# Even mixing part of a two-layer recurrent decoder: where the state sums over values and the pair sums stand in TensorE's order

## The chip, the cores and the metric

The kernel runs on one core of a Trainium2 chip. The metric is the device time of one execution in microseconds (us), less is better. Engines are named as the profile names them: PE is TensorE (PEld its weight loads), DVE is VectorE, ACT is ScalarE, POOL is GpSimd, SP the engine that issues most transfers.

## What is computed

A prompt of 2048 positions and a sample group of 8 x 8 positions go through two layers that share all weights. The even layer runs retention heads and RWKV-7 heads side by side from one input projection; both feed one output projection. Only the RWKV part touches the change:

```python
def rwkv7_recurrence(r, log_decay, k, v, kk, a, S0):
    def step(S, inp):
        r_t, lw_t, k_t, v_t, kk_t, a_t = inp
        s_kk = jnp.einsum('bhvk,bhk->bhv', S, kk_t)
        S = (S * jnp.exp(lw_t)[:, :, None, :] - s_kk[..., None] * (kk_t * a_t)[:, :, None, :]
             + v_t[..., None] * k_t[:, :, None, :])
        return S, jnp.einsum('bhvk,bhk->bhv', S, r_t)
...
    kk = l2norm(hd(kr * k_k))
...
    y = y + jnp.sum(r * kr * r_k, -1, keepdims=True) * vr
```

The squared lengths for `l2norm` and the sums over r * kr * r_k are sums over the 64 channels of a head: the kernel calls them pair sums, since two heads share the 128 partitions of a channel block.

## The kernel before

Four phases run one after the other: `project_phase` for the even layer, `mix_even_phase`, `project_phase` for the odd layer, `mix_odd_phase`. The change is in `mix_even_phase`.

There the sequence is cut into 17 tiles of 128 positions (PT = 16 is the index of the last, the sample tile). The recurrence inside a tile is written as a triangular system. Its inverse is built by doubling, in levels of 2, 4, 8, 16, 32 and 64; at each level PE makes X (`level_X`), DVE masks or copies it, PE makes T (`level_T`), ACT copies it out. The work is a software pipeline written out by hand: each engine walks through the same `STEPS`, a tuple (p, t, n, m, q) of tiles one apart. In one step tile p is projected out (`project`, eight pieces of six matmuls of 512 columns), tile t = p + 1 is solved and updates the state, the inverse of tile n = t + 1 is built, tile m = n + 1 gets its factors, sums and keys, and tile q = m + 1 its low-rank input. Tiles outside 0 to 16 are None, so the first steps have no p; in those, `keep_clock(count)` issues dummy matmuls on the identity where the pieces of `project` would be.

Every engine executes its list in order. Engines wait for one another by semaphores (`await_(engine, name, tile)`). PSUM is eight banks with the names A_, B_, C_, D_, BX, BY and BC (two banks); several functions take turns on each.

What the change touches in PE's list of a step, in the order of the kernel before:

- `level_T(n, 2)`, `solve(t)` (inverse times right side, into B_), `state_of_values(t)` (keys times values, the first half of the state update, into D_, four column blocks for each half of the partitions), `level_X(n, 4)`, `project(p, 0)`, `outputs_of_solved(t)` (waits for `wv_ready`, DVE's scaled copy of what `solve` made), `state_of_solved(t)` (the second half of the state update, accumulated on the first in D_), `level_T(n, 4)`.
- `project(p, 5)`, `turn_factors(m)` (twelve transposes into A_, B_, D_), `level_T(n, 32)`, `project(p, 6)`, `sums(m)` (pair sums into D_), `project(p, 7)`, `turn_sums(m)` (turns the copied sums, into D_), then `ret_scores`, `level_X(n, 64)`, `key_scores(m)` (into C_ and D_), `level_T(n, 64)`, `ret_out`, `low_rank`, `ret_delta`, `turn_mix(t)`, and the next step begins with `right_side`, `level_X(n, 2)`, `outputs_of_values`, `level_T(n, 2)`.

On ACT, `token_major(m)` copies the three turned banks to SBUF (tokB, tokK, tokV, the last from D_; event `tok_written`), then comes `level(n, 32)`, then `copy_sums(m)` (event `sums_copied`). On DVE `lengths(m)` takes what `turn_sums` made (event `lengths_ready`).

Of the kernel before, what the change touches and what calls it, by code (L numbers as in the profile page):

```python
# [8 lines left out]
ACT = mybir.ActivationFunctionType  # L9
# [3 lines left out]
P = 128  # L13
# [4 lines left out]
PT = SEQ // P  # L18
# [664 lines left out]
Q = 32  # L683
# [47 lines left out]
def mix_even_phase(nc, t_in, out):  # L731
# [6 lines left out]
    with ctx:  # L738
        def sb(n, shape):
            return ctx.enter_context(nc.sbuf_tensor(f"me_{n}", shape, F32))  # L740
# [20 lines left out]
        pair = sb("pair", [P, Q])  # L761
# [66 lines left out]
        head_sums = z[:, 0:2, :]  # L828
# [14 lines left out]
        A_, B_, C_, D_, BX, BY, BC = bk[3], bk[4], bk[2], bk[6], bk[7], bk[1], (bk[0], bk[5])  # L843
# [68 lines left out]
        def await_(eng, name, n):  # L912


            if n >= 0:
                eng.wait_ge(E[name], n + 1)
# [278 lines left out]
        def _(act):  # L1195
            def A(o, i, f, **kw):
                return nc.scalar.activation(o, i, f, **kw)
# [87 lines left out]

            def copy_sums(m):
                await_(act, "pair_sums_ready", m)
                A(head_sums, D_[:, 0:2 * P].rearrange("p (k c) -> p k c", k=2), ACT.Copy).then_inc(E["sums_copied"], 1)

            def level(n, b):  # L1290
                if level_count(n, b) is None:
# [423 lines left out]
        def _(pe):  # L1715
            def mm(o, l, r, start=True, stop=True):
                return nc.tensor.matmul(o, l, r, start=start, stop=stop)  # L1717

            def turn(o, i):
                return nc.tensor.transpose(o, i, ident)  # L1720

            def keep_clock(count):

                for _ in range(count):
                    mm(BC[0][:, 0:P], ident, ident)
# [51 lines left out]
            def state_of_values(t):  # L1779
                await_(pe, "mixT_written1", t - 1)  # L1780
                for b in range(4):
                    for half in range(2):
                        p0 = 64 * half
                        o = D_[p0:p0 + 64, b * WN:(b + 1) * WN]
                        mm(o, tokK[t % 2][:, b, p0:p0 + 64], tokV[t % 2][:, 2 * b + half, :], start=b == 0, stop=False)
# [8 lines left out]
            def state_of_solved(t):  # L1794
                for b in range(4):
                    for half in range(2):
                        p0 = 64 * half
                        last_op = mm(D_[p0:p0 + 64, b * WN:(b + 1) * WN], tokB[t % 2][:, b, p0:p0 + 64], wv[:, 2 * b + half, :], start=False, stop=b == 3)
                        if b == 3:
                            last_op.then_inc(E[f"delta{half}_ready"], 1)  # L1800
# [78 lines left out]
            def receptance_scores(n):  # L1879
                await_(pe, "mga_read", n)  # L1880
                low_side(n, 1, (A_, B_), "g2")
# [34 lines left out]
            def sums(m):  # L1916
                await_(pe, "squares_ready", m)
                await_(pe, "bonus_in", m)
                await_(pe, "tok_written", m)
                for k, src in enumerate((sq, z)):  # L1920
                    for b in range(4):
                        last_op = mm(D_[b * Q:(b + 1) * Q, k * P:(k + 1) * P], pair[:], src[:, b, :])
                last_op.then_inc(E["pair_sums_ready"], 1)

            def turn_sums(m):
                await_(pe, "sums_copied", m)
                for k in range(2):
                    last_op = turn(D_[:, k * P:(k + 1) * P], head_sums[:, k, :])
                last_op.then_inc(E["sums_ready"], 1)
# [114 lines left out]
            for p, t, n, m, q in STEPS:  # L2044
                if m == 0:
                    pe.wait_ge(s_c[1], 16 * N_C[1])
                last_step = p == PT
                if t is not None:
                    right_side(t)
                if n == 0:  # L2050
                    keep_clock(8)
                if n is not None:
                    level_X(n, 2)
                if t is not None:
                    outputs_of_values(t)
                if n == 0:
                    keep_clock(12)
                if n is not None:
                    level_T(n, 2)
                if t is not None:  # L2060
                    solve(t)
                    if t < PT:
                        state_of_values(t)
                if n is not None:
                    level_X(n, 4)
                if p is not None and not last_step:
                    project(p, 0)
                elif p is None and n is not None:
                    keep_clock(4)
                if t is not None:  # L2070
                    outputs_of_solved(t)
                    if t < PT:
                        state_of_solved(t)
                if n == 0:
                    keep_clock(8)
                if n is not None:
                    level_T(n, 4)
                if p is not None and not last_step:
                    project(p, 1)
                elif p is None and n is not None:  # L2080
                    keep_clock(4)
                if n is not None:
                    key_side(n, "a")
                    level_X(n, 8)
                if p is not None and not last_step:
                    project(p, 2)
                elif p is None and n is not None:
                    keep_clock(6)
                if n is not None:
                    key_side(n, "b")  # L2090
                    level_T(n, 8)
                if p is not None and not last_step:
                    project(p, 3)
                elif p is None and n is not None:
                    keep_clock(4)
                if t == PT:
                    for r in range(2):
                        sample_ret_state(1, r)
                if n is not None:
                    level_X(n, 16)  # L2100
                    receptance_scores(n)
                    turn_q_k(n)
                    if n == 0:
                        keep_clock(8)
                    level_T(n, 16)
                if p is not None and not last_step:
                    project(p, 4)
                elif p is None and n is not None:
                    keep_clock(4)
                if t == PT:  # L2110
                    sample_wk_state(0)
                if n is not None:
                    level_X(n, 32)
                if p is not None and not last_step:
                    project(p, 5)
                elif p is None and n is not None:
                    keep_clock(4)
                if m == 0:
                    keep_clock(24)
                if m is not None:  # L2120
                    turn_factors(m)
                if n is not None:
                    level_T(n, 32)
                if p is not None and not last_step:
                    project(p, 6)
                elif p is None and n is not None:
                    keep_clock(4)
                if t == PT:
                    sample_wk_state(1)
                if m == 0:  # L2130
                    keep_clock(5)
                if m is not None:
                    sums(m)
                if p is not None and not last_step:
                    project(p, 7)
                elif p is None and n is not None:
                    keep_clock(4)
                if t == PT:
                    sample_wk_state(2)
                if m is not None:  # L2140
                    turn_sums(m)
                if n is not None:
                    ret_scores(n)
                    level_X(n, 64)
                if m is not None:
                    key_scores(m)
                if n is not None:
                    level_T(n, 64)
                    ret_out(n)
                if q is not None:  # L2150
                    low_rank(q)
                if n is not None and n < PT:
                    ret_delta(n)
                if t is not None:
                    turn_mix(t)
                if t == PT:
                    sample_wk_state(3)
                if last_step:
                    for part in range(KD):
                        project(p, part)  # L2160
# [1238 lines left out]
```

## Time and profile before

| what | value |
|---|---|
| time, median of 3 runs | 3091.2 us (3082.86 to 3097.23) |
| profiled execution, its own time | 3089.68 us |
| its span | 3087.9 us, 85694 instructions |
| PE busy over the span | 2990.2 us (97%) |
| DVE / ACT / POOL busy | 1917.3 / 994.2 / 486.3 us |
| mean granted clock of TensorE | 0.982 |

The span is what the trace covers; the execution's own time is 1.8 us more. The even mixing phase lies between about 706 and 1546 us of the span. A busy PE in these rows means that a matmul was in flight; since matmuls overlap, the distance from one start to the next says more than the duration.

### The profile page before, as it was taken

What the parts mean: (1) busy time and instruction counts of PE and PEld (TensorE: products, weight loads), DVE (VectorE), ACT (ScalarE), POOL (GpSimd) and SP (SyncE); (2) the same over time, 40 slices, a digit from 0 to 9 for tenths busy, and PEclk for the clock granted to TensorE, in tenths of its full rate; (3) what the DMA queues carried; (4) which work ended last, traced back from release to release, by engine and by line L of the source; (5) the groups of instructions that cost most, each with busy time, mean ns of one, the idle gap of its engine ahead of it and who ended that gap; (6) DMA issues with size and microseconds to landing.
All of it is one profiled execution on the core that took longest, in us unless ns stands there. A gap on an engine that the chain in (4) does not pass through costs nothing. (4 is left out here: it accounts for less than half of the span.)

```text
span 3087.9 us, 85694 instructions
## 1 busy us (share of the span) xinstructions
PE 2990.2 (97%) x37108; PEld 2713.4 (88%) x37108; DVE 1917.3 (62%) x3976; ACT 994.2 (32%) x2170; POOL 486.3 (16%) x503
## 2 busy tenths in 40 slices
PE   9999999997999999999989999999996999999998
PEld 9999999996888888888789999999995788788886
DVE  4322244445777777777444266776765788788886
ACT  4221100003344344333166122222223344444441
POOL 0000000002343343333300000000001111111112
PEclk9999999998999999999899999999998999999999
DMA  6431122215233343333342222122114223333333
GB/s 217 142 91 69 60 91 69 69 57 182 76 121 103 114 121 113 117 121 124 104 171 90 82 73 77 61 77 77 61 64 154 84 84 98 93 97 97 98 105 130
DMA packets 216617, 311.45 MB, mean 101 GB/s; under 512 B 33449, under 2 KB 156081, under 8 KB 216113
## 3 DMA queue, kind: packets, MB, share of 16 engines
q1 hardware_dynamic: 203904, 260.76, 26.3%
q0 software_dynamic: 7872, 28.95, 3.1%
q10 hardware_dynamic: 4464, 16.25, 1.9%
q8 instruction: 294, 4.82, 0.7%
q14 instruction: 83, 0.67, 0.1%
HBM read 210.18 MB, written 95.72 MB: 99 GB/s over the span
## 5 line engine op out<-in xcount | busy, mean ns | idle before, releaser
L619 PE MATMUL po_ps<-po_xnT_hi,po_rounded 128*128 128x424 f32 x1920 | 389.6, 355 | 0.0
L619 PEld LDWEIGHTS po_ps<-po_xnT_hi,po_rounded 128*128 128x128 f32 x1920 | 361.2, 188 | 8.9
L619 PE MATMUL pe_ps<-pe_rounded,pe_xnT_hi 128*128 128x410 f32 (+1 forms) x1360 | 270.8, 350 | 2.3 <-ACT pe_xnT_hi L328 1.6
L444 DVE SCALAR_TENSOR_TENSOR po_stage<-po_area,po_cw,po_stage 128x424 f32<-128x424 f32 (+2 forms) x432 | 246.2, 584 | 27.9 <-issue 1.3
L619 PEld LDWEIGHTS pe_ps<-pe_rounded,pe_xnT_hi 128*128 128x128 f32 x1360 | 254.2, 189 | 5.8 <-ACT pe_xnT_hi L328 2.2
L619 PE MATMUL pe_ps<-pe_xnT_hi,pe_rounded 128*128 128x424 f32 x1040 | 210.4, 354 | 0.0
L328 ACT ACTIVATE po_area<-po_ps 128x424 f32<-128x424 f32 (+1 forms) x192 | 72.9, 394 | 409.9 <-PE po_ps L619 408.3
L619 PE MATMUL po_ps<-po_xnT_lo,po_rounded 128*128 128x424 f32 x960 | 204.4, 355 | 0.0
L619 PEld LDWEIGHTS pe_ps<-pe_xnT_hi,pe_rounded 128*128 128x128 f32 x1040 | 195.4, 188 | 4.5
L619 PEld LDWEIGHTS po_ps<-po_xnT_lo,po_rounded 128*128 128x128 f32 x960 | 180.5, 188 | 4.5
L520 DVE TENSOR_SCALAR po_stage<-po_area,po_cw 128x424 f32<-128x424 f32 x144 | 56.0, 403 | 142.4 <-ACT po_area L328 142.3
L619 PE MATMUL pe_ps<-pe_rounded,pe_xnT_lo 128*128 128x410 f32 (+1 forms) x680 | 142.0, 350 | 0.0
L619 PE MATMUL po_ps<-po_rounded,po_xnT_hi 128*128 128x348 f32 (+1 forms) x816 | 140.7, 325 | 0.0
L229 POOL DMA_DIRECT2D po_area<-in_w_in_o x56 | 29.7, 537 | 659.0 <-PE po_ps L619 649.3
L619 PEld LDWEIGHTS po_ps<-po_rounded,po_xnT_hi 128*128 128x128 f32 x816 | 131.7, 190 | 0.0
L494 DVE TENSOR_TENSOR pe_area<-pe_ps,pe_area 128x424 f32<-128x424 f32 (+1 forms) x65 | 38.1, 586 | 146.2 <-PE pe_ps L619 146.1
L444 DVE SCALAR_TENSOR_TENSOR pe_stage<-pe_stage,pe_ps 128x206 f32<-128x206 f32 (+2 forms) x51 | 26.0, 510 | 165.4 <-ACT pe_stage L328 165.4
L328 ACT ACTIVATE pe_stage<-pe_ps,pe_rstd 128x410 f32<-128x410 f32 (+2 forms) x85 | 43.6, 533 | 264.2 <-PE pe_ps L619 261.8
L619 PEld LDWEIGHTS pe_ps<-pe_rounded,pe_xnT_lo 128*128 128x128 f32 x680 | 127.6, 189 | 0.7 <-DVE pe_xnT_lo L470 0.3
L1717 PE MATMUL me_b<-me_w_hi,me_mixT 128*128 128x512 f32 x272 | 121.5, 447 | 2.4 <-DMA me_ring<-scratch_w_lo 1.4
L229 POOL DMA_DIRECT2D pe_area<-in_w_in_e x44 | 23.9, 548 | 605.9 <-PE pe_ps L619 597.3
L3003 PE MATMUL mo_b<-mo_w_hi,mo_mixT 128*128 128x512 f32 x272 | 118.4, 435 | 0.8 <-DVE mo_mixT_lo L2679 0.4
(450 smaller groups left out, 6451.2 us busy)
## 6 DMA issues: line engine op xcount, KB each, us to landing
me_ring<-scratch_w_lo SPq DMA_DIRECT2D x68, 512.0 KB, 3.9
mo_c<-scratch_ch_o SPq DMA_DIRECT2D x51, 512.0 KB, 3.8
scratch_ch_o<-po_stage SPq DMA_DIRECT2D x96, 212.0 KB, 1.9
scratch_tok_e<-pe_stage SPq DMA_DIRECT2D x68, 205.0 KB, 3.0
me_xs<-scratch_ch_e SPq DMA_DIRECT2D x17, 768.0 KB, 6.3
po_area<-in_w_in_o POOLq DMA_DIRECT2D x48, 256.0 KB, 3.9
scratch_ch_e<-pe_stage SPq DMA_DIRECT2D x52, 212.0 KB, 1.9
me_g<-scratch_tok_e SPq DMA_DIRECT2D x17, 512.0 KB, 3.9
```

What stands on the lines that cost most here:

```text
L229: eng.dma_start(raw[u][:, i * HK:(i + 1) * HK, :], w_in[:, at:at + HK * n].rearrange("p (k n) -> p k n", k=HK)).then_inc(loaded(r)[0], 16)
L328: return nc.scalar.activation(o, i, f, **kw)
L444: return nc.vector.scalar_tensor_tensor(out=o, in0=a, scalar=s, in1=b, op0=op0, op1=op1)
L494: last = nc.vector.tensor_tensor(to[:, HALO + c * CHN:HALO + c * CHN + w], ps[:, 0:w], rstd_row[:, c * CHN:c * CHN + w], ALU.mult)
L520: last = nc.vector.tensor_scalar(o, src, k, None, ALU.mult, ALU.bypass)
L619: last = nc.tensor.matmul(out, left.bitcast(F32R), right.bitcast(F32R), start=(i == 0 and k == 0), stop=(i == 2 and k == KD - 1))
L1717: return nc.tensor.matmul(o, l, r, start=start, stop=stop)
L3003: return nc.tensor.matmul(o, l, r, start=start, stop=stop)
```

## The change

`state_of_values(t)` moves from behind `solve(t)` to between `outputs_of_solved(t)` and `state_of_solved(t)`. `sums(m)` moves from between the pieces 6 and 7 of the projection to ahead of both, directly behind `level_T(n, 32)` (`sample_wk_state(1)`, and for m = 0 five dummies, stand between where they exist); it writes C_ in place of D_, so that it waits for the copy of the turned queries and keys of the tile before out of C_ (`qkT_written`), and no longer for `tok_written`; that wait goes to `turn_sums`. In steps without p the two groups of four dummies become one of eight.

```diff
             def copy_sums(m):
                 await_(act, "pair_sums_ready", m)
-                A(head_sums, D_[:, 0:2 * P].rearrange("p (k c) -> p k c", k=2), ACT.Copy).then_inc(E["sums_copied"], 1)
+                A(head_sums, C_[:, 0:2 * P].rearrange("p (k c) -> p k c", k=2), ACT.Copy).then_inc(E["sums_copied"], 1)
...
             def sums(m):
                 await_(pe, "squares_ready", m)
                 await_(pe, "bonus_in", m)
-                await_(pe, "tok_written", m)
+                await_(pe, "qkT_written", m - 1)
                 for k, src in enumerate((sq, z)):
                     for b in range(4):
-                        last_op = mm(D_[b * Q:(b + 1) * Q, k * P:(k + 1) * P], pair[:], src[:, b, :])
+                        last_op = mm(C_[b * Q:(b + 1) * Q, k * P:(k + 1) * P], pair[:], src[:, b, :])
                 last_op.then_inc(E["pair_sums_ready"], 1)
 
             def turn_sums(m):
                 await_(pe, "sums_copied", m)
+                await_(pe, "tok_written", m)
...
                 if t is not None:
                     solve(t)
-                    if t < PT:
-                        state_of_values(t)
...
                 if t is not None:
                     outputs_of_solved(t)
                     if t < PT:
+                        state_of_values(t)
                         state_of_solved(t)
...
                 if n is not None:
                     level_T(n, 32)
-                if p is not None and not last_step:
-                    project(p, 6)
-                elif p is None and n is not None:
-                    keep_clock(4)
                 if t == PT:
                     sample_wk_state(1)
                 if m == 0:
...
                 if m is not None:
                     sums(m)
                 if p is not None and not last_step:
+                    project(p, 6)
                     project(p, 7)
                 elif p is None and n is not None:
-                    keep_clock(4)
+                    keep_clock(8)
```

## Rows read from the trace of the kernel before

**Rows 1.** Window over two full steps: PE, PEld, DVE, ACT, POOL busy (instructions), clock, DMA.

```profile
1098.00:1187.00 89.00, 88.76 (x1837) 74.74 (x1837) 68.80 (x141) 35.74 (x82) 34.31 (x37) 1.00 0.39 118
```

**Rows 2.** Waits of PE, 690 to 1545 us: total, times, longest.

```profile
PE me_b L1717 <- issue: 7.7, 11, 1.4
...
PE me_b L1717 <- DVE me_XA L1357: 2.2, 3, 1.5
```

**Rows 3.** Timeline of PE (start us, us, instructions [idle before]): piece 6, sums, piece 7, turn.

```profile
1032.30 0.50 PE L1717 MATMUL me_b<-me_w_hi,me_mixT 128*128 128x512 f32 x1
1032.64 0.40 PE L1717 MATMUL me_b<-me_ring,me_mixT 128*128 128x512 f32 x1
...
1033.57 0.40 PE L1717 MATMUL me_b<-me_w_hi,me_mixT_lo 128*128 128x512 f32 x1
1033.90 0.43 PE L1717 MATMUL me_b<-me_sq,me_pair 128*32 128x128 f32 x8
...
1034.47 0.50 PE L1717 MATMUL me_b<-me_w_hi,me_mixT 128*128 128x512 f32 x1
...
1035.97 0.38 PE L1720 MATMUL me_b<-me_ident,me_z 128*128 128x128 f32 x2
```

**Rows 4.** Timeline of PE where a piece of the projection follows another directly.

```profile
1476.54 0.40 PE L1717 MATMUL me_b<-me_w_hi,me_mixT_lo 128*128 128x512 f32 x1
1476.78 0.40 PE L1717 MATMUL me_b<-me_w_hi,me_mixT 128*128 128x512 f32 x1
```

**Rows 5.** Timeline of PE and ACT around the sums of tile 0 (m = 0).

```profile
726.95 0.61 ACT L1197 ACTIVATE me_tokV<-me_b 128x512 f32<-128x512 f32 x1
...
727.70 0.43 PE L1717 MATMUL me_b<-me_sq,me_pair 128*32 128x128 f32 x8 [0.64 <-ACT me_tokV L1197]
...
728.40 0.38 ACT L1197 ACTIVATE me_z<-me_b 128x256 f32<-128x256 f32 x1 [0.84 <-PE me_b L1717]
728.84 0.44 PE L1720 MATMUL me_b<-me_ident,me_z 128*128 128x128 f32 x2 [0.49 <-ACT me_z L1197]
```

**Rows 6.** Timeline of PE around the state sums; 1008.52 is the last matmul of `solve`.

```profile
1001.75 0.56 PE L1717 MATMUL me_b<-me_tokV,me_MG 128*128 128x64 f32 x4
1002.26 0.74 PE L1717 MATMUL me_b<-me_TA,me_ILc 32*32 32x32 f32 x64
...
1006.11 0.74 PE L1717 MATMUL me_b<-me_XA,me_TA 32*32 32x32 f32 x64 [0.28 <-DVE me_XA L1357]
1006.82 1.97 PE L1717 MATMUL me_b<-me_rhs,me_TF 128*128 128x64 f32 x16
1008.52 0.28 PE L1717 MATMUL me_b<-me_rhs,me_TF 128*128 128x64 f32 x1
1008.72 0.69 PE L1717 MATMUL me_b<-me_tokV,me_tokK 128*64 128x64 f32 x16
1009.34 0.75 PE L1717 MATMUL me_b<-me_TA,me_ILc 32*32 32x32 f32 x64
...
1011.53 1.89 PE L1717 MATMUL me_b<-me_yw,me_G2T 128*128 128x64 f32 x16
1013.35 0.69 PE L1717 MATMUL me_b<-me_yw,me_tokB 128*64 128x64 f32 x16
1013.96 0.75 PE L1717 MATMUL me_b<-me_XA,me_TA 32*32 32x32 f32 x64
```

**Rows 7.** Timeline of DVE and ACT in the same step: what follows `level_T(n, 2)`, `solve(t)` and `level_T(n, 32)`.

```profile
1006.90 0.38 ACT L1197 ACTIVATE me_TA<-me_b 128x256 f32<-128x256 f32 x1 [3.23 <-PE me_b L1717]
...
1009.10 0.69 DVE L1357 TENSOR_TENSOR me_yw<-me_b,me_n 128x512 f32<-128x512 f32 x1
...
1034.61 0.38 ACT L1197 ACTIVATE me_z<-me_b 128x256 f32<-128x256 f32 x1 [0.47 <-PE me_b L1717]
```

**Rows 8.** Timeline of PE: the longest gap named "issue", and what follows it.

```profile
1061.06 0.32 PE L1717 MATMUL me_b<-me_XA,me_TA 32*32 32x32 f32 x14 [1.42 <-issue]
...
1062.01 0.63 PE L1717 MATMUL me_b<-me_w_hi,me_mixT_lo 128*128 128x512 f32 x1
```

## Prediction

> **What bounds the kernel now.** I read the page first: PE is busy for 97% of the span, no other engine for more than 62%. Then the windows over the even mixing phase, the only one that the diff touches. Over two full steps of it PE is in flight 88.76 of 89.00 us at the full granted clock, 1.00, that is 2.4 GHz; DVE has 68.80 us of work, ACT 35.74 [rows 1]. A step takes 44.5 us there. So in the middle of the phase nothing that only lets another engine begin earlier can show; what counts is the distance between starts on PE. Then the waits of PE for the whole phase: 7.7 us in 11 gaps named "issue", where PE waited for no other engine, and 2.2 us in 3 waits for DVE's masked X [rows 2]. Last, the timelines around the two moved calls.
>
> The reader is to see there that PE pays for a change of tile shape. A projection matmul of 512 columns starts 0.233 us after the one before (from 1032.64 to 1033.57 there are four). The first of a piece behind another kind takes 0.34, and the last, with the pair sums (128*32) behind it, 0.33: 0.10 too much at each of these ends [rows 3]. Where a piece follows a piece the distance is 0.24, so neither is paid [rows 4].
>
> **The pair sums.** Before: piece 6 takes 1.60 us (1032.30 to 1033.90), the sums 0.57, piece 7 1.50 up to the turn, 3.67 together [rows 3]. After: the sums, still 0.57, then twelve projection matmuls in one run: 0.34 for the first, 10 x 0.233, and 0.23 for the last, which has the full-size turn behind it as piece 7 has now. That is 2.90, together 3.47: 0.20 us less. The remaining question is what the sums cost directly behind the 32*32 matmuls of the level of 32. No row has that pair; piece 6 starts there without a wait, and I take the same entry for the sums. Bounds by the nearest rows: only one end of the two saved (0.10 less), or nothing lost at the entry either (0.30 less).
>
> This happens in the steps with p from 0 to 13 (m = p + 3 ends at 16), 14 times: 2.8 us. In two more steps, m = 1 and 2, dummies stand for the pieces; the groups join in the same way, and I take 0.2 us each as an estimate from the same ends: 0.4 us.
>
> At m = 0 a real wait goes. PE waited 0.64 us for tokV's copy, made the sums, and waited 0.49 us more for the copy of them [rows 5]. After the change the sums run during the three copies of ACT, and their copy can follow tokV's. That one ends at 727.56, and 0.38 us behind it the copy of the sums would end, near 727.95, where it now ends at 728.78. `turn_sums` then comes about 0.9 us earlier. PE and DVE wait for one another through this start, so I pass the 0.9 on; bounds 0 and 0.9.
>
> The new waits cost nothing that I can see. `qkT_written` of the tile before lies far back, before piece 4. `tok_written` now stands at `turn_sums`: behind it on PE are the retention scores and everything after, and DVE waits for it in `lengths`. But ACT has copied tokV and the level of 32 by 1034.14, since the copy of the sums began at 1034.61 after 0.47 us of waiting for PE [rows 7]. After the change it begins some 0.4 us earlier, and the turn stands where it did, near 1035.8. The turn had 0.98 us to spare already (1034.99 to 1035.97, [rows 3, 7]), so the earlier copy buys nothing there. If the cover of the two pieces were missing, the turn would pay the copies as at m = 0, about 1 us a step. The ring of streamed weights is freed by piece 6 some 0.5 us later and by piece 7 no later; its next use is in the next step. ACT's square root follows the copy and DVE needs it only behind `lengths`.
>
> **The state sums over values.** Before: the last matmul of `solve` starts at 1008.52, the moved call at 1008.72, `level_X(n, 4)` at 1009.34: 0.82 us. The moved call is eight pairs of matmuls, one on each half of the columns; its row ends at 1009.41, and with some 0.2 us for one matmul the last pair began near 1009.18, so a pair takes 0.065 us. After: the last of `solve` has 32*32 matmuls behind it. The same passage, full size to 32*32, stands at 1001.75: four matmuls of 0.56 us, one of which lasts 0.28, so the last began at 1002.03 and the 32*32 came at 1002.26, 0.23 later [rows 6]. The moved call, in one run with `state_of_solved`, costs its eight pairs, 0.52 us. Together 0.75 for 0.82: 0.07 us less, 16 times (t from 0 to 15): 1.1 us. Bounds: 0 (what is saved at one end is paid at the other) and 0.14 (pairs at 0.055): 0 to 2.2 us.
>
> Its cover goes too. The 0.62 us stood between the level of 2 and `level_X(n, 4)`, which needs ACT's copy of T. That ends at 1007.28, and `level_X(n, 4)` would now start near 1008.75: 1.4 us to spare. `outputs_of_solved` waits for DVE's yw, which begins at 1009.10 and ends at 1009.79; PE would be there at 1011.53 - 0.6 = 1010.9, 1.1 us to spare [rows 6, 7]. If the cover were gone, the lack would be paid in full. The delta of the state is ready when it was, so DVE's new state, POOL and the next right side see no shift.
>
> At both places the rule in the Trainium skill, "TensorEngine Tiling (Array Packing)", section Tiling Modes, Key Properties, is that a change of tiling mode makes the array drain while another tile of the same mode does not. The ends of 0.10 us and the joined pieces agree with it [rows 3, 4]. By the rule alone the sums' move takes away one change of mode of three per step, and the other move one of six; at 0.10 us each this is 0.2 x 16 = 3.2 us, against 4.3 us (2.8 + 0.4 + 1.1) by the rows.
>
> **The sum.** 2.8 + 0.4 + 0.9 + 1.1 = 5.2 us off the profiled execution: 3089.7 - 5.2 = 3084.5 us. That execution is 1.5 us below the median of the runs, so the median would be 3086.0 us. Bounds of the terms: at least 1.6 (0.10 x 16), at most 4.8 + 0.9 + 2.2 = 7.9 us. The three runs before spread from 8.3 below their median to 6.0 above, more than the gain. A measurement of this kernel can tell about 0.5%, 15.5 us, from no change.
>
> **Rivals.**
> - **A: a pure reordering.** What the switches cost is paid elsewhere (the entry of the sums behind 32*32, of the level behind `solve`), and the start's 0.9 us ends in another wait. PE then does the same work in the same time: 3091 us. For it: 97% busy, and no wait for another engine is removed in a full step. Against it: the measured ends of the pieces.
> - **B: the DVE chain sets the step.** From the turn to `level_T(n, 2)` DVE has almost no pause, and PE waited 0.28 us for its masked X at 1006.11 [rows 6]; over the phase PE waited 3 times [rows 2]. Both moves lie outside this stretch, so what they save should come through. Where it did not, each step would pay up to 0.28: 16 x 0.28 = 4.5 us back, about 3090 us.
> - **C: slower, by gaps in the supply of instructions.** Gaps named "issue" sit inside runs of many small matmuls: one of 1.42 us, after which projection matmuls took 0.63 in place of 0.40 us, on the slow clock level by their spacing [rows 8]. The gap and what follows cost about 3 us (1.42 and some eight matmuls at 0.2 us more). The change puts the sums (16 matmuls) right behind the 48 of the level of 32, and takes the slower `state_of_values` from between the bursts of the levels 2 and 4. If this emptied the supply in each of 16 steps at the mean 0.7 us of the gaps [rows 2], it would be 11.2 - 5.2 = 6.0 us more: 3097 us. To be slower by 0.5% it needs 15.5 + 5.2 = 20.7 us, seven of the long kind. Against it: the sums are few, and the burst of 64 pairs is unchanged.
> - **D: a hidden cover.** The wait for the sums' copy is longer in many steps than in the one I read, and the 0.57 us of the sums was hidden as well: 14 x 0.57 = 8.0 more, 3078 us. Against it: PE shows a wait for that copy once, at m = 0. Faster by 0.5% would need 1 us in each step, of which no row shows a sign.
>
> **How the numbers follow.** My forecast (3.5 to 8 us less) 0.62; A 0.15; B 0.08; C 0.09, of which 0.02 beyond 0.5%; D 0.06, of which 0.03 beyond, with the scatter of a median of few runs. That scatter can carry my own case beyond 0.5% too, by some 0.02. So faster 0.05, within 0.5% 0.92, slower 0.03. The range: D at its lower end and A to C with the scatter of the runs at its upper end, 3078 to 3096 us. The forecast's own terms alone give 3083 to 3090.
>
> **What would show it.** A step of 44.2 us in place of 44.5 in the middle of the phase; the two pieces 6 and 7 in one run of 2.9 us; the sums starting 0.1 us behind the level of 32; from the last matmul of `solve` to `level_X(n, 4)` 0.23 us and the 32 state matmuls in about 1.1 us; at m = 0 no wait for tokV before the sums. The prediction is wrong if PE shows waits for yw or for T's copy, if the sums cost more than 0.6 us behind the 32*32 matmuls, or if the "issue" gaps grow by more than a few us.

## The result, and the profile of the kernel after

The changed kernel takes 3074.6 us (median of 11 runs, 3069.54 to 3086.18) beside 3089.5 us for the kernel before (11 runs, 3080.16 to 3097.23): ratio 0.9949, interval 0.9934 to 0.9964, so 0.51% faster. In a second comparison of the same two kernels it took 3076.0 beside 3090.3 us: 0.9957 (0.9938 to 0.9976). I had forecast 5.2 us less; it is 13 to 16 us less, below the lower end of my range. The interval of these 11 runs reaches about 5 us to either side: they can tell a change a third as large as the 15.5 us that I had thought was needed. The profiled execution took 3073.24 us. Every execution timed here ran at a mean granted clock of about 0.98, except one of the seven of the kernel with 256 waits further down (4196.6 us at 0.639), which is left out of its median and ratio.

The page of the kernel after, its head and the busy time of the engines:

```profile
span 3071.4 us, 85711 instructions
...
PE 2976.2 (97%) x37108; PEld 2707.2 (88%) x37108; DVE 1914.8 (62%) x3976; ACT 991.8 (32%) x2170; POOL 485.8 (16%) x503
```

The matmuls are as many as before. The 17 instructions more (85711 for 85694) are waits of PE: `turn_sums` now has two waits, once for each of the 17 tiles. Hold on to this number.

PE's timeline around the pair sums, in the same step as [rows 3]:

```profile
1029.38 0.43 PE L1717 MATMUL me_b<-me_sq,me_pair 128*32 128x128 f32 x8
1029.63 0.40 PE L1717 MATMUL me_b<-me_z,me_pair 128*32 128x128 f32 x8
1029.96 0.50 PE L1717 MATMUL me_b<-me_w_hi,me_mixT 128*128 128x512 f32 x1
...
1032.62 0.39 PE L1717 MATMUL me_b<-me_w_hi,me_mixT_lo 128*128 128x512 f32 x1
1032.85 0.38 PE L1720 MATMUL me_b<-me_ident,me_z 128*128 128x128 f32 x2
```

The sums take 0.58 us (1029.38 to 1029.96) and the pieces 6 and 7 in one run 2.89 us (to 1032.85); I had 0.57 and 2.90. The turn has no wait. Around the state sums, answering to [rows 6]:

```profile
1003.90 0.74 PE L1717 MATMUL me_b<-me_XA,me_TA 32*32 32x32 f32 x64 [0.28 <-DVE me_XA L1357]
1004.61 1.97 PE L1717 MATMUL me_b<-me_rhs,me_TF 128*128 128x64 f32 x16
1006.51 0.75 PE L1717 MATMUL me_b<-me_TA,me_ILc 32*32 32x32 f32 x64
...
1008.70 1.89 PE L1717 MATMUL me_b<-me_yw,me_G2T 128*128 128x64 f32 x16
1010.52 0.69 PE L1717 MATMUL me_b<-me_tokV,me_tokK 128*64 128x64 f32 x16
1011.04 0.64 PE L1717 MATMUL me_b<-me_yw,me_tokB 128*64 128x64 f32 x16
1011.61 0.75 PE L1717 MATMUL me_b<-me_XA,me_TA 32*32 32x32 f32 x64
```

From the start of `solve` to `level_T(n, 4)` it is 7.00 us (1004.61 to 1011.61), where it was 7.14 (1006.82 to 1013.96, [rows 6]): 0.14 less. Neither T's copy nor yw is waited for.

A full step, from one `solve` to the next where no gap falls into it, takes 43.92 us; before it took 44.27. The 15 steps from the `solve` of tile 0 to that of tile 15 took 672.9 us and now take 667.4, 5.5 less. So the even mixing phase gave about what the forecast had. Where are the other ten? From the start of the first to the last matmul of each phase, with a second profiled execution of each kernel:

| phase | before | before, second | after | after, second |
|---|---|---|---|---|
| even projection | 695.6 | 695.3 | 693.0 | 694.6 |
| even mixing | 842.3 | 837.5 | 838.2 | 835.8 |
| odd projection | 778.1 | 778.9 | 778.9 | 779.2 |
| odd mixing | 724.5 | 727.3 | 714.3 | 722.4 |

(The matmuls of the even mixing phase before run from 708.7 to 1551.0 us of the span, some 5 us further than I wrote above; no further gap of [rows 2] lies there.)

The largest difference stands in the odd mixing phase, which the diff does not touch. PE's waits there, 2336 us to the end, have two kinds that fell in the first pair of profiles, "issue" and one wait for DVE's XA (total, times, longest). Before:

```profile
PE mo_b L3003 <- issue: 10.0, 14, 2.8
...
PE mo_b L3003 <- DVE mo_XA L2746: 1.5, 1, 1.5
```

After:

```profile
PE mo_b L3000 <- issue: 5.6, 12, 1.1
```

(The wait for XA is 0.3 us there.)

The gap of 2.8 us has a tail. PE's timeline of the kernel before, seventh odd step:

```profile
2631.18 0.22 PE L3003 MATMUL mo_b<-mo_XA,mo_TA 32*32 32x32 f32 x2
2634.22 0.25 PE L3003 MATMUL mo_b<-mo_TA,mo_XA 32*32 32x32 f32 x4 [2.82 <-issue]
2634.40 1.18 PE L3006 MATMUL mo_b<-mo_ident,mo_c 128*128 128x128 f32 x8
2635.51 1.97 PE L3003 MATMUL mo_b<-mo_TB,mo_IL 64*64 64x64 f32 x16
```

In the middle of a burst of small matmuls PE has nothing to do for 2.82 us. For 6.8 us behind it the granted clock is at its half level, 1.2 GHz: the sixteen 64*64 matmuls take 1.97 us where they take 1.13 elsewhere. The same burst in the kernel after has a gap of 0.81 and the full clock, 2.4 GHz:

```profile
2622.91 0.21 PE L3000 MATMUL mo_b<-mo_XA,mo_TA 32*32 32x32 f32 x1 [0.81 <-issue]
...
2624.19 1.13 PE L3000 MATMUL mo_b<-mo_TB,mo_IL 64*64 64x64 f32 x16
```

From its first matmul of `mo_tokV,mo_TF` to that of the next, this step took 45.58 us before; a clean one takes 38.39. The 7.2 us are the gap of 2.82, another of 0.93 earlier in the step, and 3.4 us for 6.8 us at half the clock.

**Where the gaps stand.** I counted PE's instructions (weight loads, matmuls and waits, from 0) in order through each trace, and wrote down the number of the one that comes after each "issue" gap of the odd mixing phase:

| kernel | instructions behind a gap |
|---|---|
| before | 49089, 50625, 53698, 53953, 55489, 58818, 59073, 60354, 63938, 65217, 65473, 68801, 70082 |
| before, second | 49089, 49346, 50625, 52417, 54210, 55489, 59073, 60354, 63938, 65217, 68546, 68801, 70082, 74177 |
| after | 50881, 52417, 54209, 57282, 59074, 60610, 62145, 65473, 67010, 70081, 71873 |
| after, second | 49090, 50881, 52417, 54209, 55745, 57282, 60353, 60610, 62145, 65218, 65473, 67010, 71873 |

(Those of 0.15 us or more. The gap of 2.82 us is the one at 59073.) Each number is a multiple of 256, plus 193 or 194. This also holds in the even phase: the gap of [rows 8] stands before instruction 21442 in all four. Two gaps are of another kind: one of 0.89 us in the even phase (before 38419 in the kernel before, 38436 in the kernel after) and one of 0.21 us in the odd phase (49629 and 49646) stand ahead of the same matmul in every trace, and so move by 17 with it. Which points open a gap repeats largely from one execution to the next; how long it gets varies. The page's row of transfers for instructions (packets, MB, share) fits a supply in blocks of 256: 294 packets of 16384 bytes, which is 64 bytes for each of 256 instructions.

```profile
q8 instruction: 294, 4.82, 0.7%
```

PE has 75286 instructions in the kernel before, 294 full blocks. With 256 waits more (a kernel further down) the row shows one packet more:

```profile
q8 instruction: 295, 4.83, 0.7%
```

The times of these packets in the traces tie the gaps to them. Counted from 0, the point b x 256 + 193 stands in block b. In all 14 traces together there are 309 gaps at such points, and at each of them the last packet that had begun before PE went on was number b - 1. It had ended 1.2 to 1.6 us before PE went on in 307 of the 309 (0.8 and 1.0 us in the other two), whether the gap was 0.2 or 2.8 us long. Behind 2631.18 us in the rows above, packet 229 began only at 2631.96, 0.56 us into the gap, and ended at 2632.92; PE went on at 2634.22.

So the 17 waits, added in the even phase, shift all later code by up to 17 instructions against the points where a gap can come. Theory L: about half of the gain is this shift. Rival O: all of it comes from the new order, in a way that I had priced too low, and the odd phase differs by chance. The experiments separate the two.

### The profile page after: what moved, and what is told of

The parts are those of the page before. It is cut to its first block and busy times, and to the rows that moved or that the text cites. A ratio compares the mean times of both kernels' runs of the same rounds, so it can differ in the third digit from the quotient of the medians.

```text
span 3071.4 us, 85711 instructions
## 1 busy us (share of the span) xinstructions
PE 2976.2 (97%) x37108; PEld 2707.2 (88%) x37108; DVE 1914.8 (62%) x3976; ACT 991.8 (32%) x2170; POOL 485.8 (16%) x503
```

## The experiments

All times are medians beside the kernel before on the same chip; "odd mixing" is from its first to its last matmul in one profile. The ratio with its interval is not the quotient of the two medians, and the two ways differ by some us: the added waits alone are 9.0 us less by the ratio and 5.8 by the medians (3083.6 for 3089.4). Where nothing else is said, the text goes by the ratio.

| kernel | time, us | ratio (interval) | clean even step | odd mixing |
|---|---|---|---|---|
| the added waits alone | 3083.6 | 0.9971 (0.9954 to 0.9989) | 44.28 | 715.5 |
| 17 waits ahead of the odd phase | 3084.2 | 0.9973 (0.9956 to 0.9990) | as before | 723.7 |
| the new order without the waits | 3081.2 | 0.9976 (0.9951 to 1.0000) | 43.92 | 722.2 |
| pair sums alone | 3077.0 | 0.9955 (0.9934 to 0.9976) | 44.07 | 716.7 |
| state sums alone | 3085.6 | 0.9987 (0.9966 to 1.0007) | 44.12 | 732.8 |
| sums early, accumulator D_ | 3093.1 | 1.0003 (0.9988 to 1.0019) | 45.13 | 714.9 |
| sums in two halves | 3083.7 | 0.9976 (0.9956 to 0.9997) | 44.26 | 713.8 |
| after, 49 waits ahead of the odd phase | 3084.2 | 0.9980 (0.9961 to 0.9999) | as after | 715.8 |
| after, 128 waits | 3092.7 | 0.9991 (0.9969 to 1.0014) | as after | 722.1 |
| before, 256 waits | 3117.2 | 1.0080 (1.0052 to 1.0108) | as before | 716.8 |
| after, again | 3076.0 | 0.9957 (0.9938 to 0.9976) | 43.92 | 722.4 |
| before, again (one execution) | 3087.9 | | 44.27 | 727.3 |

**The added waits alone.** The kernel before with the second wait in `turn_sums`. It waits for something that `sums` has waited for already, so it never holds PE.

```diff
             def turn_sums(m):
                 await_(pe, "sums_copied", m)
+                await_(pe, "tok_written", m)
```

> The order of the kernel before; one wait more per tile on TensorE (turn_sums waits for tok_written too, long satisfied), so that the instructions of TensorE behind it stand where those of the changed kernel stand. Theory of the place of instructions (the part of the gain outside the moved calls comes from where TensorE's code stands against the points at which its supply breaks off): 8 to 10 us less than before, about 3080 us, nearly all of it in the odd mixing phase, whose gaps named issue stand at the instructions at which they stand in the changed kernel. Theory of chance (the long gap of the odd phase is a matter of one execution): within 2 us of before. Theory of the order (all comes from the moved calls): no change.

Measured: 0.9971, which is 9.0 us of 3089.4, with the interval well below 1. The even step is unchanged, 44.28 us. The odd phase has nine gaps at the points of 256, before 49090, 50881, 52417, 54209, 55490, 55745, 57282, 67010 and 71873. Eight are numbers of one of the two profiles of the kernel after; 55490 is one of the kernel before. Rival O falls: a line that does nothing gives about half of the gain (9.0 of 15.8 us by the ratios, 5.8 of 14.9 by the medians).

**The new order without the waits.** The kernel after, less that line.

```diff
             def turn_sums(m):
                 await_(pe, "sums_copied", m)
-                await_(pe, "tok_written", m)
```

> The order of the changed kernel without the wait for tok_written in turn_sums, which the wait for the sums' copy implies (ScalarE makes it behind tokV's copy); TensorE's code in the odd phase then stands as before. Theory of the place: 8 to 10 us of the gain are lost, about 3084 us, 5 to 6 us less than before. Theories of chance and of the order: as the changed kernel, 15 us less than before, 3074 us.

Measured: 0.9976, 7.4 us less, with the step of the kernel after (43.92 us) and an odd phase of 722.2 us, whose nine gaps stand at numbers of the kernel before (54210, 55489, 59073, 60354, 63938, 65217, 68801, 70082), but for one at 63681. The two halves add up: 9.0 + 7.4 = 16.4 us, and both together gave 15.8 (0.0051 x 3089.5). Each interval reaches 5 to 8 us to either side, so the sum is consistent and not exact; by the medians it is 5.8 + 8.1 for 14.9.

**Seventeen waits in another place.** The kernel before, with satisfied waits at the start of the odd mixing phase. An instruction carries two of them, so that 34 more make 17 instructions. They lie under the 18 us that PE waits there for DVE anyway.

```diff
-            pe.wait_ge(s_t, 16 * N_T)
+            for _ in range(35):
+                pe.wait_ge(s_t, 16 * N_T)
```

> The kernel before with 17 instructions more for TensorE at the start of the odd mixing phase, each a wait that is already satisfied, in a place where TensorE waits 18 us for VectorE anyway. Order and even part are as before. Theory of the place of instructions: the odd phase takes what it takes in the changed kernel and in the run with more waits, 715 us from its first to its last matmul and not 722 to 733, so about 6 us less than before, 3083 us, and gaps named issue at the same instructions as in the changed kernel. Theory that the 17 waits in the even part themselves help (by the turn's place or the start): no change, 3089 us.

Measured: 0.9973, 8.3 us less. The timed runs agree with theory L: it is the number of instructions ahead that counts, not where they stand. Of its 15 gaps in the odd phase 11 stand at numbers of the kernel after, among them 50881, 52417, 54209, 57282, 62145, 67010 and 71873. But the profiled execution was a long one, 3092.79 us, with an odd phase of 723.7 where I expected about 715; its gaps were at the right places and longer, 11.9 us in 16. A single profile shows where the gaps are, not what they cost on the mean. With this one, the profiles with the code where the kernel before has it give 722.2, 724.5, 727.3 and 732.8 us, mean 726.7; the seven with the shift of 17 give 713.8 to 723.7, mean 717.3. That is 9.4 us, beside 8.3 and 9.0 from the timed runs.

Over all the profiles the points sort by the shift. Those at 50881, 52417, 57282 and 67010 open in all seven with the shift of 17, and in the four without it only 52417, once, for 0.16 us. Those at 55489, 59073, 63938, 65217, 68801 and 70082 open in all four without it, and in the seven at most three times each.

By these profiles, what the shift is worth is for the most part time at the half clock, and not the gaps themselves. The "issue" gaps of the odd phase sum to 8.9 us on the mean of the four and to 7.2 on that of the seven. In the second odd step PE waits for DVE's XA: unbroken for 1.49, 1.77, 1.58 and 1.58 us in the four, while in the seven a gap of 0.70 to 0.97 us at 50881 comes shortly before, and 0.29 us of that wait or less is left. Two rows of PE, from the kernel before (second) and from the one with the added waits alone:

```profile
2429.54 0.21 PE L3003 MATMUL mo_b<-mo_XA,mo_TA 32*32 32x32 f32 x1 [1.77 <-DVE mo_XA L2746]
```

```profile
2432.10 0.18 PE L3004 MATMUL mo_b<-mo_XA,mo_TA 32*32 32x32 f32 x1 [0.29 <-DVE mo_XA L2747]
```

Behind the unbroken wait the granted clock fell to 1.2 GHz in three of the four, for 13.7, 6.8 and 13.7 us. From 30 us behind the phase's first matmul on, PE was at 1.2 GHz for 6.8, 13.7, 10.2 and 27.3 us in the four (mean 14.5), and for 0, 6.8, 3.4, 6.8, 0, 0 and 0 us in the seven (mean 2.4). At half the clock half of such a stretch is lost, so as an estimate from these rows this is 6 of the 9.4 us. The timed executions agree in kind: their mean granted clock is 0.981 for the kernel before (35 runs) and 0.982 with the waits alone (12 runs).

**Each move by itself.** Pair sums alone (with their waits, so with the shift) and state sums alone (without).

```diff
                 if t is not None:
                     solve(t)
+                    if t < PT:
+                        state_of_values(t)
...
                     if t < PT:
-                        state_of_values(t)
                         state_of_solved(t)
```

> Only the pair sums move (other accumulator, ahead of pieces 6 and 7, wait for tok_written in turn_sums). By the clean steps of the two traces the sums' share of the saving is 0.20 to 0.25 us a step, 3 to 4 us. Theory of the place: the odd phase stands nearly as in the changed kernel, so 3 to 4 and 8 to 10, together 12 us less, 3077 us. Theories of chance and of the order: 4 us less by the former; 10 or more by the latter, with steps shorter by 0.6 us or more.

> Only the state sums over values move; no wait is added. By the prediction 0.07 us a step, by the traces 0.10 to 0.15: 1 to 2.5 us less than before. Theory of the place: nothing more, since the code of the odd phase stands as before: 3088 us. Theory of the order: what the sums do not give, 5 us or more.

The diff stands against the kernel after and gives the pair sums alone. Their step is 44.07 us, 0.20 less than before; with the state sums alone it is 44.12, 0.15 less. Together they make 0.35, as measured. In time: 13.9 us less with the shift, and 4.0 us less without it, the latter with an interval from 10.5 us less to 2.2 us more. Less the 9.0 us of the shift, the pair sums gave 4.9. The profile of the state sums alone had the longest odd phase of all, 732.8 us, with a gap of 2.8 us in the same burst as the kernel before and 27.3 us at the half clock.

**The other accumulator.** The kernel after with the sums in D_ again, so that they wait for tokV's copy at the new place.

```diff
...
             def sums(m):
...
-                await_(pe, "qkT_written", m - 1)
+                await_(pe, "tok_written", m)
...
-                        last_op = mm(C_[b * Q:(b + 1) * Q, k * P:(k + 1) * P], pair[:], src[:, b, :])
+                        last_op = mm(D_[b * Q:(b + 1) * Q, k * P:(k + 1) * P], pair[:], src[:, b, :])
```

> The changed kernel, but the pair sums stay in the accumulator of before, so that at their new place TensorE must wait for tokV's copy. By the trace of the changed kernel that copy ends 1.06 us after the sums start, so each step is 1.0 to 1.1 us longer and 14 to 16 us are lost: 3089 to 3091 us, with a wait of TensorE for tokV in every step. If another cover hides it (rival): 3075 us.

PE's waits in its even mixing phase (total, times, longest):

```profile
PE me_b L1717 <- ACT me_tokV L1197: 18.7, 17, 1.1
```

One wait for every tile, 1.1 us each, and the step goes from 43.92 to 45.13 us. It is no faster than before (1.0003) although it has the shift. So the early place pays only with C_: with D_ the wait costs six times the 0.20 us that the place saves.

**Sums in two halves.** The sums over squares ahead of piece 6, those over z between the pieces 6 and 7: two more changes of tile shape in a step, with the same work (where dummies stand for the pieces, they are divided in the same way).

```diff
...
                 if m is not None:
-                    sums(m)
+                    sums(m, 0)
                 if p is not None and not last_step:
                     project(p, 6)
...
+                if m is not None:
+                    sums(m, 1)
+                if p is not None and not last_step:
                     project(p, 7)
```

> The changed kernel with one half of the pair sums ahead of piece 6 and the other between the pieces 6 and 7: two changes of tile shape more in each step, no wait more. Theory of the switches (0.10 us for each end of a run of full-size matmuls): clean steps of 44.1 to 44.2 us in place of 43.93, about 3 us more, 3078 us. Theory that the place of the sums as such, or their earlier copy, gave the gain: none of it is lost.

PE's timeline of that kernel:

```profile
1028.74 0.43 PE L1717 MATMUL me_b<-me_sq,me_pair 128*32 128x128 f32 x8
1029.10 0.50 PE L1717 MATMUL me_b<-me_w_hi,me_mixT 128*128 128x512 f32 x1
...
1030.37 0.40 PE L1717 MATMUL me_b<-me_w_hi,me_mixT_lo 128*128 128x512 f32 x1
1030.69 0.42 PE L1717 MATMUL me_b<-me_z,me_pair 128*32 128x128 f32 x8
1031.05 0.50 PE L1717 MATMUL me_b<-me_w_hi,me_mixT 128*128 128x512 f32 x1
...
1032.55 0.38 PE L1720 MATMUL me_b<-me_ident,me_z 128*128 128x128 f32 x2
```

From the sums to the turn it is 3.81 us (1028.74 to 1032.55), in the kernel after 3.47 (1029.38 to 1032.85); the step is 44.26, 0.34 more. I had expected 0.2. The two ends at the projection matmuls cost what I had priced (0.34 for the first, 0.32 for the last), and the sums themselves pay too: 0.36 us for either half, where they take 0.25 and 0.33 in one run.

**More waits, at other distances.** The kernel after with 49 and 128 more instructions ahead of the odd phase, on top of its own 17, the kernel before with 256, the edit being that of the 17; and both kernels once more.

> The changed kernel with 49 instructions more for TensorE at the same place. The even part stays as in the changed kernel (840 us less 4 to 8). Theory of the place: the odd phase changes by some us in a direction that the theory does not give, between 705 and 730 us, and its gaps move to other instructions; a time below 3072 us would make this the fastest version. Theory of the order: 3074.6 us, unchanged.

> The changed kernel with 128 instructions more at the same place, half a period. Theory of the place: the time differs from the changed kernel's by up to 10 us, in a direction that is not given; with 49 it was 9 us more. Rival (49 more was chance): the changed kernel's time, 3075 us.

> The kernel before with 256 instructions more for TensorE at the start of the odd mixing phase (17 there took 8 us off). The gaps of all traces so far stand a whole multiple of 256 instructions of TensorE apart, give or take one. Theory of the place, with this period: a shift by 256 puts the gaps back to where they are in the kernel before, inside the same runs of 32*32 matmuls, and the time is that of before, 3089 to 3092 us, up to a few us more if the 256 waits take longer than the 18 us they have. If any shift of this size helps, or if more instructions there are what helps (rival): 6 us or more are gained, as with 17.

> The changed kernel once more, on the same chip as the kernels beside it. All theories: 14 to 16 us less than before. The odd phase should again take 713 to 717 us from first to last matmul.

> The kernel before, one execution with a profile. Theory of the place: its gaps in the odd phase stand at the instructions at which they stood in the first trace, above all the long one inside the level of 32 of the seventh step; the odd phase takes 722 to 733 us. Theory of chance: the gaps stand elsewhere.

These waits, two to an instruction, are not free. PE's first matmul of the odd mixing phase, with the idle time before it, in the kernel before with 256:

```profile
2378.65 0.77 PE L3003 MATMUL mo_b<-mo_gall,mo_tab_p 128*128 128x128 f32 x2 [43.93 <-issue]
```

and in the kernel after with 128:

```profile
2359.42 0.76 PE L3000 MATMUL mo_b<-mo_gall,mo_tab_p 128*128 128x128 f32 x2 [29.82 <-issue]
```

The idle time is 18.0 us without them and with 17, 21.45 with 49, 29.82 with 128 and 43.93 with 256: about 0.11 us for each instruction (43.93 - 29.82 = 14.1 for the last 128). So the 256 cost 25.9 us by themselves, which I had expected to be a few us; the kernel took 24.7 us more by its ratio (0.0080 x 3090.3) and 26.9 by the medians. What is left, 1.2 us less or 1.0 more, is no measurable change, as theory L wants for a shift by a whole 256. The gaps bear it out: all ten that it has in the odd phase at these points (49345, 50881, 54466, 55745, 59329, 60610, 64194, 65473, 69057, 70338) stand exactly 256 above gaps of the two profiles of the kernel before, so ahead of the same matmuls. Its wait for XA in the second odd step is unbroken again, 1.77 us:

```profile
2457.43 0.18 PE L3003 MATMUL mo_b<-mo_XA,mo_TA 32*32 32x32 f32 x1 [1.77 <-DVE mo_XA L2746]
```

The odd phase of that profile, 716.8 us, is nevertheless as short as one with the shift of 17: in this execution the clock did not fall behind that wait, nor anywhere later in the phase. So the gaps follow the place of the code, and the time of one profile also hangs on whether the clock falls.

The kernel after with 128 took 16.7 us more than without by the medians and 10.5 by the ratios; 11.8 are the waits, so for the place of the code 4.9 us more or 1.3 less is left, and nothing can be told from it. With 49, ten gaps stand in the odd phase: three at points of the kernel after (52418, 62146, 71874, give or take one), three at points of the kernel before (49089, 49346, 68545) and four at points that neither opened (52674, 62402, 67265, 72130). Of 6.2 us less than before, 3.4 are to be added for the waits: 9.6 less, where the kernel after had 13 to 16. These intervals overlap too. So of all the shifts only the one of 17 has a gain that the timed runs show.

The two kernels once more: the odd phase of the kernel after took 722.4 us where I expected 713 to 717, with two gaps of 1.8 us, each followed by 3.4 us at the half clock. The kernel before took 727.3, and the long gap of 59073 came again, with 0.89 us in place of 2.82.

## Why the prediction was wrong, step by step

- **The pair sums: right.** 0.20 us in a step was forecast, and 44.27 - 44.07 = 0.20 measured; the 0.58 us behind the level of 32 show that no entry is paid there beyond what I took. In the steps of m = 1 and 2, from the last 32*32 matmul to the turn, it is 2.58 us for 2.89, 0.31 less each where I had estimated 0.2.
- **The state sums: right in kind, mis-sized by half.** I had 0.07 us, it is 0.14 to 0.15. The moved call took the 0.52 us that I gave it (1010.52 to 1011.04). Its neighbour got shorter as well, 0.57 us (1011.04 to 1011.61) for 0.61 [rows 6], and the passage from `solve` to the level of 4 cost no more than the one to the moved call had: from the first matmul of `solve` it is 1.90 us in both kernels. This makes the term 0.14 x 16 = 2.2 us, the upper bound that I had written for it.
- **The start at m = 0: 0.9 us forecast, 0.7 there at equal clock, 0.1 in the profiled execution.** PE's timeline there, for [rows 5]:

```profile
723.88 1.93 PE L1717 MATMUL me_b<-me_ident 128*128 128x128 f32 x10
725.73 0.42 PE L1717 MATMUL me_b<-me_sq,me_pair 128*32 128x128 f32 x8
...
726.88 0.44 PE L1720 MATMUL me_b<-me_ident,me_z 128*128 128x128 f32 x2 [0.50 <-ACT me_z L1197]
```

  The wait for tokV is gone. But the ten dummies ahead of the sums ran at the half clock here, 1.93 us, where they took 1.28 before: from tokB's copy to the turn it was 2.76 us, before 2.86. The clock at this spot changes from one execution to the next. In the kernel after with 49 waits later on, whose code is the same up to here, the dummies took 1.28 us and the turn came 2.16 us after the start of tokB's copy: 0.7 us less than before. I had let the sums' copy follow tokV's at once; it still waits for the sums.
- **The even phase as a whole: right in size, in part by luck.** 2.8 + 0.6 + 2.2 + 0.1 = 5.7 us with the measured terms of this execution, for the 5.2 forecast: the state sums gave 1.1 us more than their term, and the start 0.8 less. The 15 steps from `solve` to `solve`, which leave out the start, show 5.5 (2.8 between the second profiles), scatter of their gaps included; the timed kernel without the shift gave 7.4. Four profiles with the even code of before give 837.5, 842.3, 842.5 and 847.8 us for the phase, four with that of after 835.8, 837.0, 838.2 and 840.9: means 842.5 and 838.0, 4.5 less.
- **The step that failed** stands under "The pair sums", where I wrote that the new waits cost nothing that I could see and so put them at nothing in the sum, and under rival C, where I looked for gaps in the supply only at the two places of the move, and only as a loss. I priced the waits as waits. That they are also 17 instructions, and where those put the code of the whole rest of the kernel, was in none of my cases, though [rows 2] and [rows 8] showed the gaps. That omission is 8 to 9 us less by the ratios (0.9971 and 0.9973 for 17 waits alone, in two places; 6 to 8 by the medians), with a sign that nothing in the profile of before gave.
- **The rivals.** A is refuted by the steps (0.35 us less). B is too: the wait of 0.28 us for DVE's masked X is still there, and what was saved outside of it came through. D had the right size of time for the wrong reason: no cover was hidden, only the shift made up for it. C as I put it did not come: the "issue" gaps of the even phase are 8.6 us in 12, for 7.7 in 11 [rows 2]. Its price of a long gap with the slow clock behind it stands; where such gaps fell was decided in the odd phase, at which it did not look.
- **The rule on tile shapes.** The rows of both kernels and of the split one show 0.10 us at each end of a run of projection matmuls. The Trainium skill, "TensorEngine Tiling (Array Packing)", section Tiling Modes, Key Properties, says that the array drains on a change of tiling mode; the traces agree. At 0.10 us for a change that rule gave 3.2 us, my rows 4.3, and the steps show 0.35 x 16 = 5.6: a change costs more than the one end by which I had priced it, as the halves of the sums show too.

What stays open: why the packet for some of the points comes late and for others doesn't (280 of the 309 gaps stand directly behind a 32*32 matmul, so in or just behind the bursts of small ones), what makes a gap of 0.4 or of 2.8 us at the same point, and when the clock falls behind an idle time: between 40 and 620 us of the odd phase PE was idle for 1.4 us or more at a stretch 15 times in all traces, and at 12 of them the clock fell to 1.2 GHz within 1.2 us of the end. No run changed the supply itself, and what share of the gain the gaps and the clock have is read from single profiles.

## What to carry to other kernels

Where a profile shows gaps named "issue" inside bursts of small instructions, any edit that adds or removes instructions on that engine can move the later code against the points where its supply comes late; test it by adding the same number of instructions that do nothing, before the gain is credited to the idea. Grouping matmuls of one tile shape is worth some 0.1 to 0.2 us at each end that goes, so here 0.35 us a step; it is kept only if the moved group has an accumulator that is free at its new place. A difference of half a per cent needs the timed runs: single profiles whose odd phase stood at the same place differed by 10 us in it, most of this by stretches at the half clock.

## What the runs showed of the hardware that was not expected

- In these traces PE's gaps without a waited-for engine stand at instruction numbers that are 193 or 194 above a multiple of 256, in whichever phase: 308 of 341, and one more at 195. Of the other 32, 28 are the two that stand ahead of the same matmul in all 14 traces, and three are the start of the odd mixing phase with 49, 128 and 256 waits. The transfers of instructions are 16384 bytes each, and 1.2 to 1.6 us lie between the end of the transfer for the block before and PE's next instruction in 307 of the 309.
- The gap of 2.82 us was followed by 6.8 us at a granted clock of 1.2 GHz; with another gap of 0.93 us its step took 7.2 us more than a clean one (45.58 for 38.39).
- An instruction of PE that carries two waits whose conditions have long been met costs about 0.11 us where nothing covers it: with 256 of them the idle time was 25.9 us longer.
